# Two attention blocks at the end of a network: projection weights as half-contraction units of 512 columns, and a gate activated in place

## The reference, cut to what matters

```python
# fox: 16 heads, causal with forget terms     dsw: the same with 3 groups of dilated windows, rotary q and k
proj = h @ w_in                               # fox: 1024 x (4*1024 + 16)    dsw: 1024 x (10*1024)
q, k = rms_norm(...), rms_norm(...)           # per head
o = softmax(q k' ...) v
x = x + (o * jax.nn.silu(gate)) @ w_out       # gate: the last 1024 columns of the projection
```

## Time and profile before

| | us |
|---|---|
| three runs | 2334.09, 2339.29, 2339.95 |
| median | 2339.29 |
| profiled execution: span | 2331.6 |
| profiled execution: its own device time | not listed apart from its span |
| fox and dsw, start of the first transposes to the end of the span | 1735.75 to 2331.6 |

### The profile page before, as it was taken

One profiled execution on the slowest core, in us unless ns is written; L12 is line 12 of the kernel. 1 busy time (PEld: TensorE's weight loads), 2 busy tenths in 40 slices (PEclk: granted clock), 3 DMA queues, 4 the chain that ended last, 5 costly groups with the idle time before them and its releaser, 6 DMA issues.

```text
span 2331.6 us, 49885 instructions
## 1 busy us (share of the span) xinstructions
PE 2269.8 (97%) x22220; PEld 1801.6 (77%) x22220; DVE 881.6 (38%) x1903; ACT 463.2 (20%) x853; POOL 27.2 (1%) x66
## 2 busy tenths in 40 slices
PE   8999999999999999989999999999999999999998
PEld 6888767777688877677777777877778868888884
DVE  3675642665434562322022021121123442343443
ACT  2333312000125332110000000000003341232232
POOL 2000000000000000000000000000000000000000
PEclk9999999999999999999999999999999999999999
DMA  9553255777433324549999999999963324333320
GB/s 390 200 199 128 105 220 191 278 293 276 170 140 131 133 103 145 217 180 401 402 401 401 395 402 401 403 405 404 408 254 127 109 91 156 118 124 127 109 73 19
DMA packets 75532, 538.06 MB, mean 231 GB/s; under 512 B 8552, under 2 KB 8560, under 8 KB 11440
## 3 DMA queue, kind: packets, MB, share of 16 engines
q1 hardware_dynamic: 72864, 526.14, 58.1%
q0 software_dynamic: 1360, 4.85, 0.6%
q10 hardware_dynamic: 1088, 3.81, 0.4%
HBM read 529.90 MB, written 4.85 MB: 229 GB/s over the span
## 4 chain that ended last, share of the span: by engine, by line
PE 93%; DVE 3%; ACT 2%; issue 1%; DMA 0%; DVEq 0%; ACTq 0%; SPq 0%
PE ps L901 20%; PE ps L476 17%; PE ps L432 15%; PE ps L443 11%; PE ps L925 7%; PE ps L933 4%; PE ps L744 4%; PE ps L855 3%; PE ps L519 2%; PE ps L769 2%; PE ps L1084 2%; PE ps L1038 1%; PE ps L1054 1%; ACT ring L1419 1%; DVE ring L1796 1%
## 5 line engine op out<-in xcount | busy, mean ns | idle before, releaser
L901 PEld LDWEIGHTS ps<-hT,ring 128*64 128x64 f32 x11264 | 474.8, 138 | 45.9 <-issue 41.3
L901 PE MATMUL ps<-hT,ring 128*64 128x96 f32 x11264 | 485.7, 247 | 6.9 <-DVEq L2480 4.4
L476 PE MATMUL ps<-ring,hT 128*128 128x256 f32 x1792 | 401.0, 380 | 2.7 <-DVE hT L1796 2.1
L476 PEld LDWEIGHTS ps<-ring,hT 128*128 128x128 f32 x1792 | 335.5, 190 | 52.3 <-issue 5.0
L432 PE MATMUL ps<-ring,hT 128*128 128x256 f32 x1664 | 366.0, 380 | 0.0
L432 PEld LDWEIGHTS ps<-ring,hT 128*128 128x128 f32 x1664 | 314.1, 190 | 44.6 <-issue 2.5
L1419 ACT ACTIVATE RA<-ps 128x192 f32<-128x192 f32 (+2 forms) x159 | 69.9, 440 | 1120.7 <-PE ps L901 586.8
L1796 DVE TENSOR_TENSOR RA<-ps,RA 128x192 f32<-128x192 f32 (+1 forms) x99 | 39.1, 395 | 635.8 <-PE ps L901 552.4
L443 PE MATMUL ps<-hT,ring 128*128 128x256 f32 (+1 forms) x1280 | 269.0, 370 | 0.1
L443 PEld LDWEIGHTS ps<-hT,ring 128*128 128x128 f32 x1280 | 232.0, 190 | 33.1 <-issue 3.1
L925 PE MATMUL ps<-ring,RA 128*64 128x512 f32 x704 | 168.0, 594 | 0.2 <-issue 0.2
(11 more groups left out here) (301 smaller groups left out, 1719.1 us busy)
## 6 DMA issues: line engine op xcount, KB each, us to landing
ring<-stream SPq DMA_DIRECT2D x497, 1024.0 KB, 8.9
slots_scratch<-YT ACTq DMA_DIRECT2D x7, 384.0 KB, 8.1
x_rows<-x SPq DMA_DIRECT2D x2, 512.0 KB, 13.5
gates_row<-bgate SPq DMA_DIRECT2D x1, 1024.0 KB, 19.0
QT<-bgate SPq DMA_DIRECT2D x1, 1024.0 KB, 21.0
rows_scratch<-RB ACTq DMA_DIRECT2D x2, 512.0 KB, 4.5
out<-x_rows SPq DMA_DIRECT2D x2, 512.0 KB, 2.7
rowt<-rows SPq DMA_DIRECT2D x1, 460.0 KB, 16.0
```

Source lines behind the costliest of these rows:

```text
L476: m = pe.matmul(ps[:, b, t * UC:(t + 1) * UC], hT[:, k, t * P:(t + 1) * P], ring[:, s, k * UC:(k + 1) * UC], start=k == 0, stop=k == KC - 1)
L901: m = pe.matmul(ps[64 * j:64 * (j + 1), b, c * CAP:(c + 1) * CAP], ring[:, s, k * UC + c * P + 64 * j:k * UC + c * P + 64 * (j + 1)], hT[: ...
```

## The change

Only the two last blocks change. Their weight units are laid out anew: a unit is now one half of the contraction (512 rows) by 512 columns, and two such units make a block of 512 output columns, which are two neighbouring old units (q and k of fox; v and gate; in dsw q0 q1, q2 k0, k1 k2, v0 v1, v2 gate). One token tile of a block is 8 written matmuls of 512 columns into a whole bank of PSUM, four from each unit. `wide_part` does one half of that. An item (block, tile, half) takes the place of a projection half in the steps; the number per step is unchanged. The units are streamed in plain order, so the gate comes last.

The eviction is now a plain copy of one token tile, 128x512, as soon as its bank is full (`wide_out`); the list `late` is gone. The gate's silu is applied in place later, in step 2 of the quad that uses it (`gate_silu`), with its two table switches, and DVE's `gated` waits for it on a semaphore of its own. At step 4 the root is always followed by the switch back to exp. DVE's first squares of dsw move from step 2 to step 3.

```diff
-FOX_ORDER = (0, 1, 3, 2)
-DSW_ORDER = (0, 1, 2, 3, 4, 5, 9, 6, 7, 8)
-FOX_HALVES = [[(j, t)] for j in FOX_ORDER for t in range(T)]
-DSW_HALVES = [[(DSW_ORDER[i // T], i % T) for i in range(*at)] for at in
-              ((0, 3), (3, 6), (6, 9), (9, 12), (12, 14), (14, 16), (16, 18), (18, 20))]
+FOX_STEPS = [[(b, t, kh)] for b in range(2) for t in range(T) for kh in range(2)]
+DSW_ITEMS = [(b, t, kh) for b in range(5) for t in range(T) for kh in range(2)]
+DSW_STEPS = [DSW_ITEMS[lo:hi] for lo, hi in
+             ((0, 3), (3, 6), (6, 9), (9, 12), (12, 14), (14, 16), (16, 18), (18, 20))]
+SILU_STEP = 2
...
+            def wide_part(key, at, t, kh, last, block=None):
+                if kh == 0:
+                    ticket[key, "bank", t] = next_bank("U")
+                b = ticket[key, "bank", t]
+                for k in range(kh * KH, (kh + 1) * KH):
+                    if block:
+                        block(k)
+                    m = pe.matmul(ps[:, b, :], hT[:, k, t * P:(t + 1) * P],
+                                  ring[:, at[kh], k % KH * WC:(k % KH + 1) * WC], start=k == 0, stop=k == KC - 1)
...
-                def half(qd, j, t):
...
+                def item(qd, blk, t, kh):
+                    key = (name, qd, blk)
+                    if (t, kh) in ((0, 0), (0, 1)):
+                        open_units.setdefault(key, []).append(landed_unit())
+                    wide_part(key, open_units[key], t, kh, t == T - 1)
...
-                        while late:
-                            key = late.pop()
-                            unit_full("act", [open_unit[key][1]], key)
...
+            def wide_out(name, qd, blk, t):
+                b = bank_of(act, ((name, qd, blk), t))
+                link(fn((RA, RB)[qd % 2][:, t, blk * WC:(blk + 1) * WC], ps[:, b, :], ACT.Copy), took)
+
+            def gate_silu(qd, at):
+                a = (RA, RB)[qd % 2][:, :, at * UC:(at + 1) * UC]
+                fn(a, a, ACT.Silu).then_inc(gate_made, 1)
...
                             if n == NORM_STEP:
                                 root_table()
                                 root(meansq[:, 0:16 * groups])
-                                if (gate, 1) not in halves[n]:
-                                    exp_table()
+                                exp_table()
                             if n == TURN_STEP:
                                 turned(qd + 1)
-                            for j, t_ in halves[n]:
-                                if t_ and j != gate:
-                                    quad_unit(name, qd + 1, j, gate)
+                            for blk, t_, kh in steps[n]:
+                                if kh:
+                                    wide_out(name, qd + 1, blk, t_)
...
-                        if not last_one and (gate, 1) in halves[n]:
-                            quad_unit(name, qd + 1, gate, gate)
+                        if n == SILU_STEP:
+                            gate_silu(qd, gate)
                             exp_table()
...
                 def gated(qd, t, c=step):
-                    taken((name, qd, 3 * groups))
+                    dve.wait_ge(gate_made, qd + 1 + (QUADS if groups > 1 else 0))
...
                 def quad_norm(qd, n):
-                    if n == NORM_STEP - 2:
+                    if n == NORM_STEP - 1:
                         squares(qd, 0)
```

More of the change, by code:

```diff
@@ L117, in stream_plan @@
     experts = [u for e in range(NE) for u in ffn("m", e)]
-    after = [("fox", 0, 4 * q + j) for q in range(QUADS) for j in FOX_ORDER] + [("foxo", 0, j) for j in range(4)]
-    after += [("dsw", 0, 10 * q + j) for q in range(QUADS) for j in DSW_ORDER] + [("dswo", 0, j) for j in range(4)]
+    after = [("fox", 0, 4 * q + j) for q in range(QUADS) for j in range(4)] + [("foxo", 0, j) for j in range(4)]
+    after += [("dsw", 0, 10 * q + j) for q in range(QUADS) for j in range(10)] + [("dswo", 0, j) for j in range(4)]
     return before, experts, after
@@ L500, in lead_units, with wide_tile, lead_wide @@
                             unit_full(who, [b], key)
+            def wide_part(key, at, t, kh, last, block=None):
[7 more added lines that the diff above has]
+                                  ring[:, at[kh], k % KH * WC:(k % KH + 1) * WC], start=k == 0, stop=k == KC - 1)
+                if last:
+                    m.then_inc(unit_done, 1)
+                if last and kh:
+                    unit_full("act", [b], (key, t))
+                elif last:
+                    done.more()
+                elif kh:
+                    finish(m, "act", [b], (key, t))
+            def wide_tile(key, at, t, last, block=None):
+                for kh in range(2):
+                    wide_part(key, at, t, kh, last, block)
+            def lead_wide(tag, key, order=(0, 1)):
+                at = [landed_unit(), landed_unit()]
+                for t in order:
+                    if t == order[1]:
+                        norm_turn(tag, t)
+                    wide_tile(key, at, t, t == order[1], lambda k: k % 4 or need((tag, t, k // 4)))
             def unit_full(who, banks, key):
@@ L1022, in experts, with attention @@
                     state["unit"] = u0 + NE * EXPERT_UNITS
-            def attention(groups, tag, name, halves, qk, val, turn, then=None):
-                at, open_unit, late = [], {}, []
+            def attention(groups, tag, name, steps, qk, val, turn, then=None):
+                at, open_units = [], {}
                 together = 2 if groups > 1 else 1
@@ L1107, in attention @@
                                 turn(qd + 1, 0)
-                            for i, (j, t_) in enumerate(halves[n]):
+                            for i, it in enumerate(steps[n]):
                                 if n == TURN_STEP and i == 1:
                                     turn(qd + 1, 1)
-                                half(qd + 1, j, t_)
-                            if n == TURN_STEP and len(halves[n]) == 1:
+                                item(qd + 1, *it)
+                            if n == TURN_STEP and len(steps[n]) == 1:
                                 turn(qd + 1, 1)
@@ L1167, in fox @@
                 norm_turn("nfox", 0)
-                lead_units("nfox", [("act", ("fox", 0, j)) for j in range(2)])
+                lead_wide("nfox", ("fox", 0, 0))
                 b = next_bank("T")
@@ L1197, in fox @@
                     turn(0, t)
-                attention(1, "foxP", "fox", FOX_HALVES, qk,
+                attention(1, "foxP", "fox", FOX_STEPS, qk,
                           lambda qd, kt, g, h: (RA, RB)[qd % 2][:, kt, 512 + h * 64:512 + (h + 1) * 64], turn, "ndsw")
             def dsw():
-                lead_units("ndsw", [("act", ("dsw", 0, j)) for j in range(2)], order=(1, 0))
-                for j in DSW_ORDER[2:]:
-                    rows_unit("act", ("dsw", 0, j))
+                lead_wide("ndsw", ("dsw", 0, 0), order=(1, 0))
+                for b in range(1, 5):
+                    at = [landed_unit(), landed_unit()]
+                    for t in range(T):
+                        wide_tile(("dsw", 0, b), at, t, t == T - 1)
                 def turn(qd, t):
@@ L1220, in dsw @@
                     turn(0, t)
-                attention(DG, "dswP", "dsw", DSW_HALVES, qk,
+                attention(DG, "dswP", "dsw", DSW_STEPS, qk,
                           lambda qd, kt, g, h: (RA, RB)[qd % 2][:, kt, (6 + g) * UC + h * 64:(6 + g) * UC + (h + 1) * 64],
@@ L1674, in ffn, with attention @@
                                       slot_rows[0:CAP, :]).then_inc(slots_free[0], 16)
-            def quad_unit(name, qd, j, gate):
-                rows_out((name, qd, j), (RA, RB)[qd % 2][:, :, j * UC:(j + 1) * UC], ACT.Silu if j == gate else ACT.Copy)
+            def wide_out(name, qd, blk, t):
[4 more added lines that the diff above has]
+                fn(a, a, ACT.Silu).then_inc(gate_made, 1)
             def exp_table():
                 link(fn(junk_a[:, 0:1], eps[:, 0:1], ACT.Exp))
-            def attention(groups, tag, name, halves, turned):
+            def attention(groups, tag, name, steps, turned):
                 gate = 3 * groups
@@ L1733, in fox @@
                     norm_sum(t)
-                for j in range(2):
-                    quad_unit("fox", 0, j, 3)
+                for t in range(T):
+                    wide_out("fox", 0, 0, t)
                 root(meansq[:, 0:16])
@@ L1753, in turned @@
                             blocks_out(("dswT", qd, t, g), D_QT[qd % 2][:, 4 * g:4 * g + 4, t * P:(t + 1) * P])
-                for j in DSW_ORDER:
-                    quad_unit("dsw", 0, j, 3 * DG)
-                    if j == 6:
+                for b in range(5):
+                    for t in (1, 0) if b == 0 else (0, 1):
+                        wide_out("dsw", 0, b, t)
+                    if b == 3:
                         root(meansq[:, 0:48])
@@ L1760, in dsw @@
                 turned(0)
```

(2 more changed lines are left out.)

36 lines of the change are left out of this document (16 added, 20 removed).

## The result

The changed kernel takes 2342.79 us (median of 7, 2340.14 to 2347.18) against 2339.29 before (7 runs): a ratio of 1.0025 [1.0014, 1.0036], 5.8 us of 2339. The forecast was 2342.4 us, 3.1 us more than before. On two further chips the same kernel gave 1.0020 [1.0008, 1.0032] and 1.0033 [1.0019, 1.0046]. The difference is thus real, small, and about twice the forecast sum: the mean of the three is 6.1 us. The profiled execution took 2341.58 us with a span of 2339.8, so some 1.8 us lie around a span.

A forecast was written before the change was run, and what follows sets the result against it. PE was taken as the bound, busy for 97% of the span. Matmuls -2.2 us and step 4 stalls +5.3 us, all else 0, gave +3.1 on 2339.3, so 2342.4 us; range 2334 to 2351.

The forecast's parts named there:

- The matmuls: Fox and dsw: 896 wide matmuls replace 1792 narrow ones, 2.5 ns less for a pair, 2.2 us saved.
- the halved weight loads: Fox and dsw: half the weight loads go, worth nothing because PE never waits for them in a run.
- Step 4 of dsw: Table switch and projection eviction ahead of the transposes' eviction keep PE still 1.77 us longer in three quads, 5.3 us.
- The silu in place: End of step 2, eight times: 3.4 us of ACT, hidden, counted 0, up to 0.4 us if the activation takes 0.94.
- The prologues: Silu and two loads leave them; dsw's chain to DVE's scaled q gets shorter, but ACT's exp load follows: no gain.
- The rule of the Trainium skill: Drain of about 1.38 us at each table load; forecast rejected it; as a rival 2349.2 us, chance 0.02.
- Sum: Whole kernel: -2.2 us of matmuls and +5.3 us of stalls give +3.1 us, 2342.4 us.
- the term for the clock: Whole kernel: granted clock read as at the upper level (2.4 GHz) in all forty slices; nothing for it entered the sum.

The follow-up runs named there:

- narrow: Changed kernel with each matmul of 512 columns again split into two of 256; ratio to the kernel before 1.0029 [1.0018, 1.0041].
- before_switch: Kernel before with one edit: in step 4 of dsw the switch back to exp comes right behind the root; ratio to the kernel before 1.0016 [1.0006, 1.0025].
- switch_late: Changed kernel with the switch back to exp in step 4 of dsw behind the transposes' evictions; ratio to the kernel before 0.9994 [0.9983, 1.0005].
- no_silu: Changed kernel without silu on the gate of both blocks and its two table switches; ratio to the kernel before 1.0018 [1.0009, 1.0027].
- double: Changed kernel with two further table switches behind the root in step 4 of dsw; ratio to the kernel before 1.0094 [1.0081, 1.0107].
- filled: Changed kernel with four added matmuls of 256 columns, results unread, where PE waits in step 4 of dsw; ratio to the kernel before 1.0020 [1.0011, 1.0028].
- tightened: Changed kernel with step 4's switch late, dsw prologue's exp load right behind its root, projection evictions after first transposes' in steps 4 to 7; ratio to before 0.9985.
- double_b: The kernel of `double`, changed kernel plus two further table switches in step 4 of dsw, timed again on another chip; ratio to the kernel before 1.0082 [1.0065, 1.0098].

## Why the prediction was right, and what it missed

- **The matmuls**, -2.2 us: measured by the pair of groups (396.2 and 398.4 us) and by `narrow`. That the halved weight loads were worth nothing isn't shown by itself: no run changes them without the width, and both together gave the 2.2 us.
- **Step 4 of dsw**, +1.77 three times: the steps grew by 1.77, 3.36 and 1.76. Its parts hold one by one: the switch alone 1.13 (`before_switch`), the eviction alone 0.25 (`switch_late`), and both together more than their sum, since each alone is first covered by the 0.4 us that ACT had free there.
- **The silu in place**, 0: `no_silu`.
- **The prologues**, 0: fox -0.5 all in, that is its share of the pitch. In dsw the wait for DVE did go, and ACT's load then held PE up about as long, as the forecast had it. The prologue there was 1.3 shorter, of which 0.4 is pitch; the rest is a clock drop that the kernel before had there in its profile (0.80 and 0.77 granted in the two stretches from 2000 to 2008) and the changed one had not.
- **The rule of the Trainium skill** on a drain of 1.38 us behind each table load ("ScalarE: Activation LUTs", What ACT_TABLE_LOAD costs): the traces don't agree. The load at 2154.22 begins 0.02 us after the root and the next activation 0.02 after its end. `double` added two switches and 3.0 us of wait (1.95 to 4.98), not 5.3.
- **What failed is the step "Sum"**: it took the stall's price for its length. The measured +4.7 to +7.7 us are the 3.1 of the queue and a loss to the clock that is 3.0 and 4.0 us above that of the kernel before in the two comparisons where it was measured. With each execution's loss taken off its time, the changed kernel is 2.2 and 3.9 us over the kernel before (standard error 0.6 each), 3.0 on the mean: the queue's sum stands, and the term for the clock was put at nothing. The nines in all forty slices had been read as a clock that was always at its upper level, but a slice shows 9 from 90% on, and the mean granted clock of that same execution was 0.995, some 12 us of loss. The drops behind the three stalls make about 1.6 us of the 3.0 and 4.0 (5 in 15, 1.6 us each). Where the other 1.4 and 2.4 us (standard error 1.1 to 1.2) lose their clock is open: the profiles have a drop of the same size in the last quad in some kernels (the changed one 5.28 us for eight wide matmuls at 2300.65, also `no_silu`, `filled`, `tightened`) and not in others, at waits that the kernel before has as well, and one profile of each can't tell whether the change made it likelier.
- The median came out at 2342.8 for 2342.4, but that is luck in part: a sum 3 us too small met a median difference (3.5 us) smaller than the ratio of its own runs.

## What to carry to other kernels

When a change puts work in front of something another engine hands back, price it by walking that engine's queue past the hand-back; this gave each step here to 0.05 us. Then ask how long TensorE stands still there: a stall of 2 us cost 1.77 us by the queue and on average another 0.5 by the clock, one of 5 us another 1.4 to 2.9 each time. Table switches belong behind the evictions that TensorE waits for, and a stall that can't be removed is cheaper with idle matmuls in it.

## What the runs showed of the hardware that I had not expected

TensorE fell from 2.4 to 1.2 GHz at a stillness of 1.95 us in 5 cases of 15, and at one of 5 us in six of six. A fall that began as TensorE went on, or later, cost about 1.6 us of work; the three of `double_b`, which began within the stillness and lasted longer, cost 1.7 to 2.9. Shorter waits close together went before falls too: in dsw's prologue of the kernel before (0.92 and 0.87 us, then 0.80 granted from 2000 to 2004), and in the last quad (1.29 and 0.75 us) in 4 of the 14 profiles. The Trainium skill ("TensorE: Matmul & The Clock Gate", HAM oscillation — how this bites in real kernels) describes a kernel that falls to the lower clock again and again because TensorE idles on waits between bursts, and the traces agree: 11 falls in 21 stalls of these two lengths in which it stood still, 0 in 9 in which it was given matmuls. Falls of the clock also make most of the scatter between executions of one kernel: over the 190 executions on record with a clock, the loss of an execution accounts for 0.7 of the variance of its time about its kernel's mean on that chip. Of the changed kernel's seven, the fastest (2340.14) had a mean granted clock of 0.993 and the slowest (2347.18) 0.990, and 0.003 of 2342 us is 7.0 us, the whole distance. Two executions can be compared to a microsecond only stage by stage, with each stage's granted clock beside it.
